# Low halves of the retention values and of both gates on GpSimd instead of VectorE, in the second block of a two-block network

## The reference, cut to what matters

```python
def hybrid_mixer(h, w_in, w_out, ret_norm_w, hgrn_norm_w, lb, cos, sin, log_gamma):
    proj = h @ w_in                       # eight slices of 512 columns
    rq, rk, rv, rg, hq, hf, hi, hg = jnp.split(proj, idx, axis=-1)
    rq = rotary(rq...); rk = rotary(rk...) * (RET_DK ** -0.5)
    r_out = retention_chunkwise(rq, rk, rv, log_gamma)
    r_out = head_norm(r_out, ret_norm_w) * jax.nn.silu(rg)
    ...
    g_out = hgrn2_chunkwise(q_h, log_f, k_in, v_h)
    g_out = head_norm(g_out, hgrn_norm_w) * jax.nn.silu(hg)
    merged = jnp.concatenate([r_out, g_out], axis=-1)
    return merged @ w_out
```

## Time and profile before

| | |
|---|---|
| median of three runs | 2557.62 us (2557.2 to 2559.9) |
| the profiled execution's own time | 2558.99 us |
| its span, first to last instruction | 2557.2 us |
| TensorE busy | 2404.0 us, 94% |
| VectorE busy | 1953.5 us, 76% |
| ScalarE busy | 1523.0 us, 60% |
| GpSimd busy | 4.4 us |
| mean granted TensorE clock | 0.961 of full speed |

### The profile page before, as it was taken

How to read it: one execution, slowest core, us unless ns; L and a number is a source line. 1 busy time by engine, 2 the same in 40 slices (tenths; PEclk the granted TensorE clock), 3 DMA queues, 4 the chain that set the end, 5 groups by cost and what they waited for, 6 DMA issues and landing times.

```text
span 2557.2 us, 39433 instructions
## 1 busy us (share of the span) xinstructions
PE 2404.0 (94%) x14884; PEld 2059.4 (81%) x14884; DVE 1953.5 (76%) x2671; ACT 1523.0 (60%) x2078; POOL 4.4 (0%) x8
## 2 busy tenths in 40 slices
PE   6998999899899999999999999996979999979998
PEld 5997999889867676777777777774978998978998
DVE  5765778786579898989898989896776887676664
ACT  4554443455367787878787878685534554534553
POOL 0000000000000000000000000000000000000000
PEclk9999999899989999999999999997989999999999
DMA  8343678545559898989898989894412667412440
GB/s 353 132 165 141 238 273 345 228 184 198 197 201 369 312 368 308 369 310 367 312 367 310 368 311 366 315 364 186 165 66 100 232 231 311 163 68 99 185 162 17
DMA packets 87982, 623.67 MB, mean 244 GB/s; under 512 B 9732, under 2 KB 11304, under 8 KB 12968
## 3 DMA queue, kind: packets, MB, share of 16 engines
q1 hardware_dynamic: 87312, 621.28, 63.7%
q10 hardware_dynamic: 536, 0.53, 0.1%
HBM read 620.72 MB, written 1.05 MB: 243 GB/s over the span
## 4 chain that ended last, share of the span: by engine, by line
PE 89%; DVE 7%; ACT 2%; issue 2%; DMA 0%; ACTq 0%; SPq 0%; DVEq 0%
PE bank L635 14%; PE bank L633 14%; PE bank L634 14%; PE bank L653 11%; PE bank L657 11%; PE bank L654 10%; PE bank L788 2%; PE bank L787 2%; PE bank L785 2%; PE bank L1043 2%; PE bank L980 1%; DVE ring_r L1541 1%; DVE Z L1550 1%; PE bank L991 1%; ACT ring_r L1160 1%
## 5 line engine op out<-in xcount | busy, mean ns | idle before, releaser
L1541 DVE TENSOR_TENSOR ring_r<-ring,ring_r 128x1024 fp32r<-128x1024 f32 x402 | 490.5, 1224 | 269.7 <-ACT ring_r L1160 269.4
L1160 ACT ACTIVATE ring_r<-ring 128x1024 fp32r<-128x1024 f32 x402 | 423.2, 1056 | 343.6 <-PE bank L657 167.5
L653 PE MATMUL bank<-XH,ring_r 128*128 128x256 f32 x2208 | 557.6, 289 | 18.8 <-DVE ring_r L1541 12.8
L654 PE MATMUL bank<-XH,ring_r 128*128 128x256 f32 x2208 | 554.5, 287 | 0.0
L653 PEld LDWEIGHTS bank<-XH,ring_r 128*128 128x128 f32 x2208 | 434.4, 197 | 21.8 <-DVE ring_r L1541 14.0
L1992 DVE TENSOR_TENSOR ring_r<-ring,Z_r 128x1024 fp32r<-128x1024 f32 x336 | 410.9, 1225 | 51.0 <-ACT Z_r L1420 51.0
L1992 DVE TENSOR_TENSOR ring_r<-ring,mhat_r 128x1024 fp32r<-128x1024 f32 x336 | 407.9, 1220 | 38.0 <-ACT mhat_r L1420 36.2
L654 PEld LDWEIGHTS bank<-XH,ring_r 128*128 128x128 f32 x2208 | 434.5, 197 | 0.1
L1420 ACT ACTIVATE mhat_r<-ring 128x1024 fp32r<-128x1024 f32 x336 | 355.9, 1061 | 111.5 <-PE bank L635 109.5
L1420 ACT ACTIVATE Z_r<-ring 128x1024 fp32r<-128x1024 f32 x336 | 356.2, 1061 | 104.5 <-PE bank L635 104.5
L634 PE MATMUL bank<-ring_r,xn_r 128*96 128x512 f32 x896 | 352.6, 394 | 0.0
(11 more groups left out here) (304 smaller groups left out, 3389.2 us busy)
## 6 DMA issues: line engine op xcount, KB each, us to landing
ring<-in_experts SPq DMA_DIRECT2D x336, 1024.0 KB, 6.8
ring<-in_stream SPq DMA_DIRECT2D x246, 1024.0 KB, 7.0
ring<-in_stream SPq DMA_DIRECT2D x6, 512.0 KB, 4.9
xT<-in_xT SPq DMA_DIRECT2D x2, 512.0 KB, 5.3
mhat<-in_memT SPq DMA_DIRECT2D x1, 1024.0 KB, 16.9
swap<-in_early SPq DMA_DIRECT2D x1, 1024.0 KB, 18.8
swap<-in_late SPq DMA_DIRECT2D x1, 1024.0 KB, 10.7
out_T<-xn SPq DMA_DIRECT2D x8, 128.0 KB, 2.0
```

The source lines that it names most:

```text
L653: pe.matmul(dst, hi[:, a], x_hi(kb), start=(n == 0), stop=False)
L654: pe.matmul(dst, lo[:, a], x_hi(kb), start=False, stop=False)
L1160: act.activation(wh(Q), raw(Q), ACT.Copy).then_inc(sems["whi"], 1)
L1541: dve.tensor_tensor(raw(Q, ring_r), raw(Q), wh(Q).bitcast(F32), ALU.subtract).then_inc(sems["wlo"], 1)
```

## The change

The twelve quarters a layer of the units rv, rg and hg get their low half from GpSimd instead of VectorE. VectorE's `low` passes over them; GpSimd subtracts those of rv before it waits for the retention scores, and those of rg and hg behind its memset. GpSimd's subtractions count on a semaphore of their own, and TensorE waits for the count of the engine that makes the quarter. The order of quarters, units and products is the same.

```diff
+        POOLED = tuple(f"b{l}.{x}" for l in range(2) for x in ("rv", "rg", "hg"))
+        low_no, lows = [], {True: 0, False: 0}
+        for nm, j, q in quarters:
+            lows[nm in POOLED] += 1
+            low_no.append(lows[nm in POOLED])
+
+        def wait_low(eng, Q):
+            eng.wait_ge(sems["wlp" if quarters[Q][0] in POOLED else "wlo"], low_no[Q])
...
+            def low(nm):
+                for q in range(4):
+                    Q = first_quarter[nm, 0] + q
+                    pool.wait_ge(sems["whi"], Q + 1)
+                    pool.tensor_tensor(raw(Q, ring_r), raw(Q), wh(Q).bitcast(F32), ALU.subtract).then_inc(sems["wlp"], 1)
+
             for l in range(2):
-
+                low(f"b{l}.rv")
                 G.wait_full(pool, f"b{l}.rS", 3)
                 pool.memset(zs(0, 2), 0.0).then_inc(sems["scz"], 1)
+                low(f"b{l}.rg")
+                low(f"b{l}.hg")
...
                 Q = first_quarter[nm, j] + q
-                pe.wait_ge(sems["wlo"], Q + 1)
+                wait_low(pe, Q)
...
                 for Q in range(at[0], at[0] + n):
                     nm, j, q = quarters[Q]
+                    if nm in POOLED:
+                        continue
                     dve.wait_ge(sems["whi"], Q + 1)
```

More of the change, by code:

```diff
@@ L319, in build @@
                    yd=4, z0=1, z1=1, z2=1, kk=1, rot=2, scz=1, dd=8, ee=8, xx=8,
-                   wu=0, whi=0, wlo=0, lb1=1, lb2=1, r1=1, r2=1, rt=1, kq=1, dc=0, ac=0)
+                   wu=0, whi=0, wlo=0, wlp=0, lb1=1, lb2=1, r1=1, r2=1, rt=1, kq=1, dc=0, ac=0)
         sems = {k: sem("s_" + k) for k in PER}
```

## The result

The changed kernel takes 2570.58 us (median of five, 2569.56 to 2572.33) against 2558.81 us for the kernel before, measured beside it: a ratio of 1.0048, 95% interval 1.0037 to 1.0060. It is slower by 11.8 us; 10.0 were forecast. The profiled execution's span is 2569.1 us against 2557.2.

What follows compares the result with a forecast made beforehand. TensorE, busy 94%, was taken to bound the kernel, waiting for VectorE before level 3. Loss 7.1 less gain 2.2, say 5.0 us a layer, twice, on 2557.62 gave 2567.6 us; 8-in-10 range 2552.5 to 2575.

Steps and rivals of the forecast that it cites:

- Part 1: rv's four quarters moved to GpSimd: no gain or loss, since TensorE waits for one semaphore as before.
- Part 2: rg's quarters leave VectorE: rv's evacuation and level 1's operands start earlier, bounded by the memset; gain 2.2 us a layer.
- Part 3: rg's quarters on GpSimd behind the memset hold up VectorE's level chain: mean loss 7.1 us a layer before the gain.
- exclusion: GpSimd's subtractions and VectorE's two-SBUF-tile instructions shut each other out wholly, from level 1 on; chance 0.48 including rival (c).
- p: Time of one GpSimd subtraction of 1024 elements, estimated at 2.25 us.
- rival (c): GpSimd wins at each level-chain instruction, p = 2.7: 8.6 us a layer slower, 2574.8 us; shares exclusion's chance of 0.48.
- Part 4: hg's four quarters moved to GpSimd: no effect, as VectorE idles behind them and TensorE needs hg only later.
- Rival (e): TensorE's clock drops after longer pauses, costing rg up to 0.7 us a layer; put into the range, no chance given.
- (a): GpSimd's reads slow VectorE little or not in the level chain; 2553.2 us with no loss; chance 0.28.
- (b): Engines share: VectorE's two-tile instructions up to level 3 stretch by half, +1.0 us a layer, 2559.6 us; chance 0.17.
- (d): GpSimd much slower, p = 4: 12.6 us a layer, hg's last quarter runs into level 4; 2583 us or more; chance 0.07.

Runs made afterwards that it cites:

- The kernel with rv and hg alone: Changed kernel with rg's low halves left on VectorE, GpSimd taking only those of rv and hg; ratio 1.0004 against the kernel before.
- the kernel in pieces: Changed kernel with each rg quarter subtracted on GpSimd in four pieces of 256 columns; ratio 1.0014 against the kernel before, 3.6 us slower.
- the reordered kernel: Kernel before, no subtraction on GpSimd, with the fourth rg quarter's low half moved behind level 3 on VectorE; ratio 0.9984, 4.1 us faster.

## Why the prediction was right

**Part 1 (rv, nothing) held.** GpSimd's last rv quarter ended at 1846.82, some 8 us ahead of its use (rv ended at 1857.6, a quarter takes 2.8). It did meet VectorE: the first product of the rotary part took 2.25 us instead of 1.22. VectorE then still waited 4.17 us for rv. The kernel with rv and hg alone shows no change.

**Part 2 (a gain of 2.2 us a layer) held to a few hundredths.** Operands of level 1 2.26 us earlier; with no GpSimd subtraction in play, 4.1 us in all. One step of it ran otherwise: I had the evacuation begin at rv's end, and it began 0.57 us ahead of that (1857.05 against 1857.62 for the last product). It was the memset alone that set the start, and VectorE waited 0.45 us for it.

**Part 3 (exclusion) held in kind and was short in size.** I had put p at 2.25 us and a loss of 7.1 us a layer; it was 8.45. The size of p was right: GpSimd's record is 2.40 us alone, and a held VectorE instruction loses 2.14 (starts 2.74 us apart instead of 0.60). What failed was the step that said when GpSimd gets in. I let it in twice a level, where VectorE pauses or works from PSUM. It gets in between any two of VectorE's two-tile instructions in a row, so all four subtractions stood in front of a two-tile instruction and none ran beside the masked copies: 4 x 2.14 = 8.6. That is rival (c), with the p of the forecast. Sum: 8.45 - 2.26 = 6.2 a layer instead of 5.0, 12.4 us against 11.8 measured. That the two agree to 0.6 us is in part luck: between the two profiled executions the first memset starts 1.90 us earlier after the change and the second 7.54 us more behind the first, of which level 3 explains 6.2. The forecast of 10.0 was 2.4 us short by this sum, 1.8 by the measured time.

The Trainium skill (SBUF — State Buffer, section Who interferes with whom) states this exclusion, for VectorE instructions with two SBUF inputs and GpSimd instructions that read. The rows agree with both halves: 0.68 us becomes 2.8 beside a subtraction and 1.0 to 1.1 beside a copy, and stays 0.68 beside memsets. That the loser waits for the whole of the other holds nearly for the subtraction (2.14 us of 2.35 to 2.40) and not for the small ones as the trace records them: 0.5 us of a piece that comes every 1.03 us, 0.3 to 0.4 of a copy that comes every 0.90. Why is open.

**Part 4 (hg, nothing) held.** The last hg subtraction ended at 1897.04 and the operands of level 4 started at 1897.02. From TensorE's first rg product to those operands it is 15.52 us in both kernels.

**Rival (e), the clock, was there and small.** The granted clock, from the table by stretches of the changed kernel:

```profile
1860.00:1867.60 7.60, 2.02 (x19) 1.83 (x17) 7.15 (x9) 1.08 (x2) 7.30 (x4) 0.92 0.55 232
1867.70:1871.70 4.00, 3.79 (x16) 3.49 (x16) 3.96 (x3) 0.00 (x0) 4.00 (x2) 0.50 0.00 0
```

Behind a pause of 5.7 us, level 1's sixteen products ran at half clock, the lower of the two levels, in 3.79 us; a level's sixteen take 2.05 at full clock. VectorE was later still, so it cost nothing there. Levels 2 and 3 of the same layer took 6.05 us together, and rg began 0.23 us later for it. In the kernel in pieces the same happened to level 3 of the second layer (3.68 us), where rg stood behind it, and cost 1.5 us.

The traces show where more of the scatter comes from. From the cross-chunk product to the first product behind the mixer (line 716) it is 55.27 and 55.25 us in the two layers before. In the reordered kernel, which has no subtraction on GpSimd, it is 53.74 us in the first layer and 56.79 in the second: the granted clock is 1.00 and 0.72 in the first 6.2 us of it, and 1.00 and 0.83 from 19.2 to 29.2 us. Before, each layer has just one of these low stretches. So each is a step of 1.5 us, and it comes and goes with the kernel and the layer. I take the rest of the scatter of 1 to 3 us between kernels to be such steps, in both directions; that is argued, not shown for each.

**Rivals (a), (b) and (d) are out:** two-tile instructions did not keep their time; stretched by half they would take about 1.0 us, and they take 2.8 one at a time; and GpSimd's 2.4 us lies far from 4.

## What to carry to other kernels

Count GpSimd's reads as VectorE's time wherever VectorE works on two SBUF tiles: 2.1 us of the faster engine for each subtraction that took it 1.2 itself. Such work is free only beside VectorE's idle time, its slack, or its work on one tile and PSUM, so ask when it starts, not how long it takes. And before work is moved to another engine, try to move the one piece that is on the path to where its own engine is idle: here that gave the whole 2.26 us a layer for a change of two numbers.

## What the runs showed of the hardware that I had not expected

- GpSimd's subtractions and VectorE's two-tile instructions take strict turns, even where VectorE's next instruction has nothing to wait for: four long instructions in a row (2.81, 2.82, 2.73, 2.83 us).
- A VectorE instruction that reads one tile and PSUM is not held at all: two masked copies take 1.35 us beside GpSimd's subtractions, as they do alone.
- A GpSimd copy that reads a single tile holds VectorE as well, by 0.3 to 0.4 us for 512 columns. Twenty memsets of the same size do not hold it.
- GpSimd's pieces of 256 columns come every 1.03 us beside VectorE (sixteen in 16.48 us), yet each holds VectorE for half a microsecond only. Splitting GpSimd's work cut its cost to VectorE from 8.45 to 4.0 us a layer, as it came less densely and in part beside the masked copies.
